# Weaving one token block's dense work between the expert row groups of the other block, in a two-block model on one core

## The chip, the cores and the metric

The kernel runs on one core of a Trainium2 chip. The metric is the device time of one launch, in microseconds (us), as the median of several runs. All data are float32. The core's engines are TensorE (PE, with its weight loads counted as PEld), VectorE (DVE), ScalarE (ACT), GpSimd (POOL) and SyncE (SP, which here issues transfers only); 16 DMA engines move data between the device's memory and the core's.

## What is computed

A batch of 256 tokens with 1024 features goes through two layers, each a mixer, then a product-key expert layer with 16 of 16384 experts for each of 8 heads, then a gated embedding (called PLE below), and after that through a second block (modulated norms, an attention of three branches, a stick-breaking attention, and a feed-forward of 2816 columns). The mixer of layer 0 is an mLSTM, that of layer 1 a latent attention (called MLA below). The expert layer is what fetches most data:

```python
def peer_ffn(x, w_q, sub_keys, u, v):
    q = (xt @ w_q).reshape(T, PEER_HEADS, 2, PEER_HALF)
    s = jnp.einsum('thcd,hcnd->thcn', q, sub_keys)
    s1, i1 = lax.top_k(s[:, :, 0], K)
    s2, i2 = lax.top_k(s[:, :, 1], K)
    ...
    top_s, top_pos = lax.top_k(cand_s, K)
    gates = jax.nn.softmax(top_s, axis=-1)
    ...
        ub = jnp.take(u, eb, axis=0)
        act = jax.nn.gelu(jnp.einsum('thkd,td->thk', ub, xb), approximate=False)
        vb = jnp.take(v, eb, axis=0)
        return jnp.einsum('thk,thkd->td', gb * act, vb)

    # first_block, for each of DEPTH = 2 layers i
        x = layer_norm(DN_ALPHA * x + mix, ln_g[i, 0], ln_b[i, 0])
        x = layer_norm(DN_ALPHA * x + peer_ffn(x, ...), ln_g[i, 1], ln_b[i, 1])
        x = x + jax.nn.sigmoid(x @ ple_w_gate[i]) * (p[i] @ ple_w_proj[i])
```

## The kernel before

Each engine runs a program written out by hand, and semaphores tie them together. So the order of the code is the order on the engine, and an engine that waits holds all that stands behind it. The 256 tokens are two token blocks (`tb` 0 and 1) of 128, one token to a partition.

**Expert rows.** A token uses 8 x 16 = 128 experts, so a block of 128 tokens has 128 gathers: each (L923, an indirect DMA that POOL issues) brings one row of 8 KB, an expert's u and v, to each partition. The four pairs of layer and block make 512 gathers. Eight row slots in `arena` (`gath`) hold them, handled in groups of two (`GRP`), four groups in flight. For a group DVE forms the two dot products with the token (L1517), ACT the gelu (`gelus`), DVE a diagonal matrix from identity, gelu and gate for each row (`diag`, L1523), and PE multiplies the diagonal by the v half of the row, 512 columns twice, into two PSUM banks (`mm`, L266), which stay open over all 128 rows. When PE is done with a row its slot is free for the next gather (`row_free`). L266 and L983 are the lines of the helpers for matmul and activation, so most PE and ACT work shows there, told apart by tiles and shapes.

**Choosing experts.** `peer(l)` first makes the queries of both blocks (16 groups of 128 columns, each for 256 tokens) and the scores. One choice (`choose`, DVE) serves two heads of one block, 32 experts, so a block has four (`UNITS`). In each layer the first two choices, both of block 0, come before the first dot product; the other six are laid in pieces, three after each group, into the rows of block 0. All weights come through `ring`, four slots of 2 MB (`take` on PE, issued by SP at L866 in the order in which PE takes them); SP waits for a slot until PE's last use of it.

**Order.** Layer 0's mixer; queries; rows of block 0; rows of block 1, with the PLE of block 0 among its first groups; then block 1's sum, norm and PLE, the MLA projections, attention and output projection of both blocks, queries of layer 1, with no rows; rows of layer 1 in the same way; PLE; the second block, here called the tail. The modulation of the tail needs products of a vector with 12 weight pieces of 512 columns (`in_w_ada`), which DVE multiplies (`ada_part`, L1307) and PE sums (`ada_sum`). Two of them (`ADA_COLS[4:6]`) stand at the output projection of the first mixer (`out_proj("mix0", ...)`), two (`ADA_COLS[6:8]`) at that of MLA, four elsewhere in the first mixer, four in the tail. The sum of the expert output with the residual is closed on PE and normed by DVE straight from PSUM.

## Time and profile before

| | |
|---|---|
| Median of 3 runs | 2393.95 us (2392.46 to 2401.32) |
| Profiled execution | 2393.88 us, its span 2392.1 us |
| PE, weight loads | 1994.0 us busy (83%), 1112.9 (47%) |
| DVE | 1355.6 us (57%) |
| ACT | 322.4 us (13%) |
| POOL | 583.3 us (24%) |
| DMA queue of the gathers (q0) | 540.13 MB, 55.0% of the engines' span |
| DMA queue of SP (q1) | 158.24 MB, 18.5% |
| Chain that ended last | PE 51%, DVE 23%, DMA 18% |

The profile is one execution of the program. Busy shares are means over a span whose stages differ, so the table alone doesn't tell what binds: that is read stage by stage, from the slices and from windows of the trace. PE's time contains matmuls at whatever clock was granted (PEclk, 1.00 is full), and a gather's time from issue to landing contains its wait behind other gathers. The gathers move 8 KB packets on one queue, the weights and vectors smaller packets on another, and both share the 16 DMA engines.

### The profile page before, as it was taken

How to read it: one execution, taken by the hardware profiler on the slowest of the kernel's cores; microseconds unless marked ns; L12 is line 12 of the kernel's file. 1: busy time of each engine (PE TensorE's matmuls, PEld its weight loads, DVE VectorE, ACT ScalarE, POOL GpSimd, SP SyncE). 2: the span in 40 equal slices, each digit the busy share in tenths (PEclk: the TensorE clock that was granted, in tenths of full speed). 3: DMA queues.
4: the chain of work that ended last, by engine and by line, in shares of the span. 5: the costliest groups of instructions: out<-in, count | busy, mean ns of one | idle time of the engine just before them, and what ended most of it. 6: DMA issues, size and time to landing. Idle time of an engine off the chain costs nothing.

```text
span 2392.1 us, 17529 instructions
## 1 busy us (share of the span) xinstructions
PE 1994.0 (83%) x6060; PEld 1112.9 (47%) x6060; DVE 1355.6 (57%) x3401; ACT 322.4 (13%) x776; POOL 583.3 (24%) x590
## 2 busy tenths in 40 slices
PE   8989777776987778989777776987777999989998
PEld 5447432332432224757432232432223877758863
DVE  3666689986566663366689986666664225420001
ACT  1111110100100001321010010100001216510000
POOL 1001344443444430001344443444432000000000
PEclk9999989899999998999989899999998989999999
DMA  7655999999999993535999999899994564233440
GB/s 262 225 193 196 393 411 401 377 393 397 369 405 422 421 421 121 200 109 221 373 410 390 392 381 422 350 397 422 421 422 160 167 220 149 78 141 112 144 176 35
DMA packets 148376, 699.49 MB, mean 292 GB/s; under 512 B 10880, under 2 KB 16064, under 8 KB 81728
## 3 DMA queue, kind: packets, MB, share of 16 engines
q0 software_dynamic: 74832, 540.13, 55.0%
q1 hardware_dynamic: 73456, 158.24, 18.5%
q8 instruction: 48, 0.79, 0.1%
q14 instruction: 40, 0.33, 0.0%
HBM read 697.28 MB, written 1.05 MB: 292 GB/s over the span
## 4 chain that ended last, share of the span: by engine, by line
PE 51%; DVE 23%; DMA 18%; ACT 3%; issue 2%; POOL 2%; DVEq 0%; POOLq 0%
PE bank L266 50%; DMA arena<-in_uv,eidx 18%; DVE arena L1517 9%; DVE sreg L1523 2%; DVE y_tok L1461 2%; POOL arena L923 2%; DVE y_tok L1457 2%; ACT glu L983 1%; DVE y_tok L1493 1%; DVE y_tok L1494 1%; DVE y_tok L1490 1%; ACT L983 1%; DVE sreg L1453 1%; ACT xT L983 1%; DVE y_tok L1453 0%
## 5 line engine op out<-in xcount | busy, mean ns | idle before, releaser
L266 PE MATMUL bank<-arena,sreg 128*128 128x512 f32 x2048 | 993.8, 636 | 318.2 <-DVE sreg L1523 317.8
L923 POOL DMA_INDIRECT arena<-in_uv,eidx x512 | 551.6, 1077 | 1165.8 <-PE bank L266 745.2
L266 PEld LDWEIGHTS bank<-arena,sreg 128*128 128x128 f32 x2048 | 396.4, 201 | 911.7 <-issue 465.1
L1517 DVE CUSTOM_DVE_ANT_0 arena<-arena,x_tok 128x1024 f32<-128x1024 f32 x512 | 619.0, 1224 | 260.7 <-DMA arena<-in_uv,eidx 258.1
L266 PE MATMUL bank<-xT,ring 128*128 128x256 f32 (+1 forms) x1984 | 447.3, 387 | 19.4 <-POOL identa L904 10.0
L266 PEld LDWEIGHTS bank<-xT,ring 128*128 128x128 f32 (+1 forms) x1984 | 379.2, 192 | 81.1 <-issue 16.1
L1523 DVE TENSOR_SCALAR sreg<-ident,glu,gate 128x128 f32<-128x128 f32 x512 | 162.3, 400 | 93.4 <-ACT glu L983 93.4
L983 ACT ACTIVATE glu<-dots 128x2 f32<-128x2 f32 x256 | 52.0, 203 | 1188.9 <-DVE dots L1517 1188.9
L266 PE MATMUL bank<-ring,xT 128*128 128x512 f32 (+4 forms) x480 | 189.6, 553 | 4.2 <-ACT xT L983 2.4
L266 PE MATMUL bank<-ring,arena 128*128 128x512 f32 x320 | 138.2, 593 | 2.6 <-ACT arena L983 2.0
L266 PEld LDWEIGHTS bank<-ring,xT 128*128 128x128 f32 x480 | 91.4, 201 | 97.0 <-issue 86.1
L983 ACT ACT_TABLE_LOAD x79 | 101.4, 1283 | 2.4 <-PEq L1908 0.8
L266 PEld LDWEIGHTS bank<-ring,arena 128*128 128x128 f32 x320 | 60.6, 190 | 78.0 <-issue 76.9
L983 ACT ACTIVATE arena<-bank 128x256 f32<-128x256 f32 (+5 forms) x118 | 50.0, 426 | 344.0 <-PE bank L266 340.4
L1848 DVE TENSOR_TENSOR arena<-arena,bank 128x256 f32<-128x256 f32 x22 | 9.3, 421 | 150.3 <-PE bank L266 150.3
L1307 DVE SCALAR_TENSOR_TENSOR ring<-ring,silu_cT 128x512 f32<-128x512 f32 x84 | 63.2, 752 | 3.0
L266 PE MATMUL bank<-arena,ring 128*128 128x256 f32 (+1 forms) x296 | 61.1, 370 | 0.7 <-ACT arena L983 0.7
L266 PE MATMUL bank<-arena 64*128 64x256 f32 (+6 forms) x304 | 56.0, 331 | 6.2 <-DVE arena L1399 4.9
L1836 DVE TENSOR_TENSOR y_tok<-bank,arena 128x512 f32<-128x512 f32 x8 | 5.5, 690 | 93.8 <-PE bank L266 93.8
L971 POOL TENSOR_SCALAR qreg<-qreg 128x384 f32<-128x384 f32 x8 | 9.3, 1167 | 198.9 <-DVEq L1767 198.7
L266 PEld LDWEIGHTS bank<-arena,ring 128*128 128x128 f32 x296 | 53.9, 202 | 7.8 <-issue 1.4
L266 PEld LDWEIGHTS bank<-arena 128*128 128x128 f32 (+2 forms) x304 | 43.1, 186 | 17.5 <-issue 7.8
(238 smaller groups left out, 969.5 us busy)
## 6 DMA issues: line engine op xcount, KB each, us to landing
ring<-in_w_ada SPq DMA_DIRECT2D x12, 2048.0 KB, 8.2
ring<-in_w_in_2r SPq DMA_DIRECT2D x10, 2048.0 KB, 11.8
ring<-in_peer_w_q SPq DMA_DIRECT2D x8, 2048.0 KB, 9.6
ring<-in_a_w_in SPq DMA_DIRECT2D x6, 2048.0 KB, 11.8
ring<-in_w_ffn_gate SPq DMA_DIRECT2D x5, 2048.0 KB, 7.8
ring<-in_w_ffn_up SPq DMA_DIRECT2D x5, 2048.0 KB, 11.0
ring<-in_w_ffn_down SPq DMA_DIRECT2D x5, 2048.0 KB, 7.9
arena<-in_uv,eidx POOLq DMA_INDIRECT x512, 11.5
```

What stands on the lines that cost most here:

```text
L266: return nc.tensor.matmul(o, l, r, start=start, stop=stop)
L923: pool.indirect_dma_start(gath[:, s, :], None, a["uv"], bass.IndirectOffsetOnAxis(ap=eidx[:, tb, it * SLOTS + s:it * SLOTS + s + 1], axis= ...
L983: return nc.scalar.activation(o, i, fn, **kw)
L1307: ins = v.scalar_tensor_tensor(w[:, k, :], w[:, k, :], scT[:, k:k + 1], w[:, k - 1, :], ALU.mult, ALU.add)
L1453: step.go(v.match_replace(scores[:, i, :], vals[:, i, 0:8], scores[:, i, :], -3.0e38))
L1457: step.go(v.max(vals[:, i, lo:lo + 8], scores[:, i, :]))
L1461: step.go(v.max_index(idx[:, i, lo:lo + 8], vals[:, i, lo:lo + 8], scores[:, i, :]))
L1490: step(v.tensor_tensor(eq, p12f[:, e, :, :].unsqueeze(3).broadcast_to([P, UH, 16, 16]), iota16[:, :].unsqueeze(1).unsqueeze(1).broadcast_t ...
L1493: step(v.tensor_tensor(eq, eq, i4[:, :, e, :].unsqueeze(2).broadcast_to([P, UH, 16, 16]), ALU.mult))
L1494: step(v.tensor_reduce(i12[:, e, :, :], eq, AX, ALU.add))
L1517: v.tensor_tensor_reduce(out=gath[:, s, 0:D], in0=gath[:, s, 0:D], in1=xt[:, tb, :], scale=1.0, scalar=0.0, op0=ALU.mult, op1=ALU.add, acc ...
L1523: v.tensor_scalar(diag[:, s, :], ident[:, :], glu[:, s:s + 1], gate[:, tb, c:c + 1], ALU.mult, ALU.mult).then_inc(sem("diag"), 1)
```

## The change

**A row's product turns round.** DVE no longer writes a diagonal. It multiplies gelu and gate of two rows (`coef`), ACT scales the v half of each row in place, and PE transposes it, eight 128 x 128 transposes a row that add up in the same two PSUM banks (L513, `is_transpose=True`). The sum is then feature-major: the residual is added by eight small matmuls, ACT moves it to `yt`, PE turns it back, and DVE norms it, with statistics and application in separate steps.

**One row of groups.** The four windows (layer 0 block 0, layer 0 block 1, layer 1 block 0, layer 1 block 1) follow each other with POOL gathering straight on. `weave` runs the same plan on PE, ACT and DVE: after the dots and the gelu of a group (`head`) come the dense slots that the plan puts there, then the product, the scaling and the transposes (`tail`).

- Window 0 carries block 1's queries and scores, and choices 1 to 7 of layer 0. Ahead of it stand only the queries of block 0 and choice 0.
- Window 1 carries, for block 0: layer 0's sum and norm, PLE, MLA projections, attention (the first 128 keys), output projection, queries of layer 1 and four choices. Window 2 carries the same for block 1, with 256 keys.
- Window 3 carries block 0's last sum, PLE and norm.
- Block 1's last sum, PLE and norm follow the rows, then the tail.

All of this is done for 128 tokens at a time, where the dense part was done for 256. So each weight from `pT_wp` to `peer_w_q` is now taken twice. The keys of the heads share a matmul shape of 128 columns; attention takes two heads at a time. PLE uses tanh of half the argument in place of the sigmoid.

**Modulation.** `ADA_COLS[4:8]` leave the two output projections for the tail: two stand at the compression matmuls, two in the attention loop. The regions `qreg` and `sreg` become `keep_region` and `work_region`, and `x_ready` and `xn_ready` become one semaphore for each block.

```diff
+PLAN = ((FIRST_SLOTS, 5, GROUPS - 4), (NEXT_SLOTS, 0, GROUPS - 2), (NEXT_SLOTS, 0, GROUPS - 2), (LAST_SLOTS, 0, 24))
+def weave(window, slots, head, tail):
+    n, lead, over = PLAN[window]
...
+        head(k)
+        upto = min(n, lead + -(-(k + 1) * (n - lead) // over))
+        while done < upto:
+            next(slots)
+            done += 1
+        tail(k)
...
 @block.tensor
-        out_proj("mix0", A["hT"], a["a_w_out"][0], ADA_COLS[4:6])
+        out_proj("mix0", A["hT"], a["a_w_out"][0])
...
+            def tail(k):
+                for e in range(GRP):
+                    s = (k * GRP + e) % SLOTS
+                    pe.wait_ge(sem("scaled"), r * PAIRS + k * GRP + e + 1)
+                    for c in range(KC):
+                        ins = nc.tensor.matmul(bank(f"pe{l}_{tb}_{c // 4}")[:, (c % 4) * P:(c % 4 + 1) * P],
+                                               gath[:, s, D + c * P:D + (c + 1) * P], ident[:, :],
+                                               start=k == 0 and e == 0 and c % 4 == 0, stop=False, is_transpose=True)
+                    ins.then_inc(sem("row_free"), 1)
...
+        for r, slots in enumerate((first_slots(), next_slots(0), next_slots(1), last_slots())):
+            start(r)
+            weave(r, slots, no_head, row_tail(r))
...
+        ada_load(ADA_COLS[4])
         w, rec = take(rows(w_in, 1536, 280), KC, 280)
...
+        ada_load(ADA_COLS[5])
         for kv in range(2):
             w, rec = take(a[f"cmp_w1_{'kv'[kv]}_2"][0].rearrange("(l p) m -> p l m", p=P), 16, P)
...
             last_use(rec, nm)
+            ada_sum(ADA_COLS[4 + kv])
...
 @block.scalar
+                act.wait_ge(sem("coef"), r * GROUPS + k + 1)
+                for e in range(GRP):
+                    s = (k * GRP + e) % SLOTS
+                    f(gath[:, s, D:2 * D], gath[:, s, D:2 * D], ACT.Copy, scale=coef[:, s:s + 1]
+                      ).then_inc(sem("scaled"), 1)
...
+            evac_T("xM", xT, tb)
+            act.dma_start(M["cg"], a["kvg"]).then_inc(sem("mla_par"), 16)
...
 @block.vector
-                for s in range(g * GRP, (g + 1) * GRP):
-                    c = it * SLOTS + s
-                    v.tensor_scalar(diag[:, s, :], ident[:, :], glu[:, s:s + 1], gate[:, tb, c:c + 1],
-                                    ALU.mult, ALU.mult).then_inc(sem("diag"), 1)
+                v.tensor_tensor(coef[:, s:s + GRP], glu[:, s:s + GRP], gate[:, tb, k * GRP:(k + 1) * GRP], ALU.mult
+                                ).then_inc(sem("coef"), 1)
```

The numbers of `PLAN` give, for each window, its slots, how many come before the rest is spread, and over how many of its 64 groups they are spread: 41, 78, 78 and 17 slots over 60, 62, 62 and 24 groups, five of the first window's 41 at its first group.

How that moves the instructions stands in the order of each engine (tile out <- tiles in, shape, count). PE before, from the rows of layer 0's block 0 (`arena,sreg`, four matmuls a row) to those of block 1, the closing sum (`x_tok,identa`), and the PLE of block 0 (`ring,xT` and `ring`):

```order
L266 MATMUL bank<-arena,sreg 128x512 x240
L266 MATMUL bank<-x_tok,identa 128x512 x2
L266 MATMUL bank<-arena,sreg 128x512 x16
L334 MATMUL bank<-ident,x_tok 128x128 x8
L266 MATMUL bank<-arena,sreg 128x512 x16
L266 MATMUL bank<-ring,xT 128x512 x8
L266 MATMUL bank<-ring 128x512 x2
L266 MATMUL bank<-arena,sreg 128x512 x16
L266 MATMUL bank<-ring,xT 128x512 x8
L266 MATMUL bank<-ring 128x512 x2
L266 MATMUL bank<-arena,sreg 128x512 x208
```

Behind it come 208 matmuls of rows with nothing between. PE after, at the same place (`ident,arena` are the rows' transposes, eight a row, sixteen a group; `ident,y_tok` is the turn of the sum):

```order
L513 MATMUL bank<-ident,arena 128x128 x736
L295 MATMUL bank<-identa,x_tok 128x128 x8
L513 MATMUL bank<-ident,arena 128x128 x16
L538 MATMUL bank<-ident,y_tok 128x128 x8
L513 MATMUL bank<-ident,arena 128x128 x48
L359 MATMUL bank<-ident,x_tok 128x128 x8
L513 MATMUL bank<-ident,arena 128x128 x16
L295 MATMUL bank<-ring 128x512 x4
L513 MATMUL bank<-ident,arena 128x128 x16
L295 MATMUL bank<-ring,xT 128x512 x4
L513 MATMUL bank<-ident,arena 128x128 x16
L295 MATMUL bank<-ring,xT 128x512 x8
```

A step of dense work now stands between almost every two groups, and it goes on like this to the window's end. SP before, the weights from layer 0's PLE to layer 1's queries, each once:

```order
L866 DMA ring<-in_pT_wp 128x2x1280
L866 DMA ring<-in_ple_w_gate 128x8x512 x2
L866 DMA ring<-in_kv_w_down_r 128x8x512
L866 DMA ring<-in_b_w_dq 128x8x384
L866 DMA ring<-in_kv_w_up 128x2x2048
L866 DMA ring<-in_b_w_uq_p 128x3x768 x2
L871 DMA lnp<-in_lnp 128x2048
L866 DMA ring<-in_b_w_out 128x8x512 x2
L866 DMA ring<-in_w_ada 128x8x512 x2
L866 DMA ring<-in_peer_w_q 128x8x512
L866 DMA ring<-in_keysT 128x2048
L866 DMA ring<-in_peer_w_q 128x8x512 x3
```

SP after, the same stretch for block 0:

```order
L992 DMA ring<-in_pT_wp 128x2x1280
L992 DMA ring<-in_ple_w_gate 128x8x512 x2
L992 DMA ring<-in_kv_w_down_r 128x8x512
L992 DMA ring<-in_b_w_dq 128x8x384
L997 DMA lnp<-in_lnp 128x2048
L992 DMA ring<-in_kv_w_up 128x2x2048
L992 DMA ring<-in_b_w_uq_p 128x3x768 x2
L992 DMA ring<-in_b_w_out 128x8x512 x2
L992 DMA ring<-in_peer_w_q 128x8x512 x2
L992 DMA ring<-in_keysT 128x2048
L992 DMA ring<-in_peer_w_q 128x8x512 x2
```

Then the same eleven rows follow once more, for block 1; the modulation's loads are gone from here. They stand in the tail, SP after:

```order
L992 DMA ring<-in_w_in_2r 128x8x512
L992 DMA ring<-in_w_ada 128x8x512
L992 DMA ring<-in_w_in_2r 128x8x280
L992 DMA ring<-in_w_ada 128x8x512
L992 DMA ring<-in_cmp_w_k 128x16x128
L992 DMA ring<-in_cmp_w_v 128x16x128
```

Before, the two compression weights (`cmp_w`) followed the `w_in` loads of 512 and 280 columns directly; now a load of `in_w_ada` stands ahead of the 280 columns and another ahead of the compression weights.

## Rows read from the trace of the kernel before

**Rows 1.** The page, part 2: granted clock and GB/s in 40 slices of 59.8 us.

```profile
PEclk9999989899999998999989899999998989999999
...
GB/s 262 225 193 196 393 411 401 377 393 397 369 405 422 421 421 121 200 109 221 373 410 390 392 381 422 350 397 422 421 422 160 167 220 149 78 141 112 144 176 35
```

**Rows 2.** Stretches: length, then busy us by engine, clock granted, DMA share, GB/s.

```profile
core 0: us, PE busy (x) PEld busy (x) DVE busy (x) ACT busy (x) POOL busy (x), PEclk, DMA share, GB/s
...
270.00:580.00 310.00, 234.83 (x465) 93.78 (x464) 260.09 (x715) 29.85 (x77) 128.18 (x116) 0.91 0.98 401
...
705.00:900.00 195.00, 144.24 (x312) 56.05 (x312) 120.44 (x235) 7.93 (x39) 79.01 (x78) 1.00 1.01 421
912.00:1110.00 198.00, 179.55 (x689) 126.34 (x688) 87.13 (x239) 45.61 (x111) 1.15 (x2) 0.93 0.37 133
...
1812.00:2392.00 580.00, 541.33 (x2250) 403.47 (x2250) 146.00 (x335) 118.23 (x256) 19.66 (x45) 0.96 0.37 132
```

**Rows 3.** DMA queues from 208.6 to 912: packets, MB, share of 16 engines.

```profile
DMA packets 40279, 276.32 MB, mean 393 GB/s; under 512 B 4160, under 2 KB 4160, under 8 KB 7488
...
q1 hardware_dynamic: 3392, 7.60, 2.9%
```

**Rows 4.** The same two queues from 275 to 300.

```profile
q0 software_dynamic: 1065, 7.73, 74.9%
q1 hardware_dynamic: 1282, 2.57, 27.3%
```

**Rows 5.** The weights' queue alone, from 300 to 330.

```profile
q1 hardware_dynamic: 913, 1.83, 16.1%
```

**Rows 6.** The gathers, line L923, over the run, from issue to landing.

```profile
DMA to landing us min/median/max: 5.5/11.5/17.7
```

**Rows 7.** The page, part 5: line, engine, tiles, shapes, count | busy, mean ns | idle.

```profile
L1517 DVE CUSTOM_DVE_ANT_0 arena<-arena,x_tok 128x1024 f32<-128x1024 f32 x512 | 619.0, 1224 | 260.7 <-DMA arena<-in_uv,eidx 258.1
...
L1523 DVE TENSOR_SCALAR sreg<-ident,glu,gate 128x128 f32<-128x128 f32 x512 | 162.3, 400 | 93.4 <-ACT glu L983 93.4
L983 ACT ACTIVATE glu<-dots 128x2 f32<-128x2 f32 x256 | 52.0, 203 | 1188.9 <-DVE dots L1517 1188.9
...
L983 ACT ACT_TABLE_LOAD x79 | 101.4, 1283 | 2.4 <-PEq L1908 0.8
```

**Rows 8.** ACT's groups by shape, same columns.

```profile
L983 ACT ACTIVATE sreg<-bank 128x512 f32<-128x512 f32 x16 | 9.6, 597 | 8.2 <-PE bank L266 8.2
...
L983 ACT ACTIVATE arena<-arena 128x1024 f32<-128x1024 f32 x5 | 5.0, 1046 | 0.0
```

**Rows 9.** PE in order of time: start, us, line, tiles, shape, count [idle before].

```profile
136.40 27.70 PE L266 MATMUL bank<-ring,arena 128*128 128x512 f32 x64 [1.03 <-ACT arena L983]
...
173.13 16.64 PE L266 MATMUL bank<-xT,ring 128*128 128x256 f32 x64 [0.99 <-ACT xT L983]
...
254.10 4.63 PE L266 MATMUL bank<-ring,qreg 128*128 128x128 f32 x40
...
919.90 1.94 PE L334 MATMUL bank<-ident,x_tok 128*128 128x128 f32 x8 [3.26 <-DVE y_tok L1276]
...
927.83 1.04 PE L334 MATMUL bank<-ident,x_tok 128*128 128x128 f32 x8
```

**Rows 10.** DVE in order of time, one expert choice, first and last instruction.

```profile
192.30 0.87 DVE L1457 MAX8 y_tok<-sreg 128x8 f32<-128x128 f32 x4 [18.99 <-ACT sreg L983]
...
208.17 0.18 DVE L1499 TENSOR_SCALAR eidx<-y_tok 128x32 uint32<-128x32 f32 x1
```

**Rows 11.** PE and DVE after the last rows, in order of time.

```profile
1854.52 5.48 DVE L1307 SCALAR_TENSOR_TENSOR ring<-ring,silu_cT 128x512 f32<-128x512 f32 x7
...
1857.30 29.76 PE L266 MATMUL bank<-xT,ring 128*128 128x256 f32 x128 [4.44 <-ACT xT L983]
...
1886.90 1.02 PE L266 MATMUL bank<-ring,ones 128*128 128x512 f32 x2
```

**Rows 12.** A stretch with a pause of the rows, columns as in rows 2.

```profile
1470.00:1500.00 30.00, 18.47 (x34) 7.47 (x33) 19.54 (x36) 3.58 (x7) 7.29 (x7) 0.77 0.87 364
```

More of the change, by code:

```diff
@@ L635, in _ @@
+        transposes("xT6", yt, KC, 1, xn_ready[1], 1)
+        for tb in range(TB):
+            await_T("xT6", tb)
         w_in = a["w_in_2r"]
```

1469 lines of the change are left out of this document (865 added, 604 removed).

## The prediction

> **What bounds the kernel now.** Read the slices first, for what is moved and when [rows 1]. They split the 2392.1 us span into five stretches. The slices near 400 GB/s are the expert rows of the two layers; in between and at the end stand dense stretches at 100 to 240 GB/s. The first choice of experts ends at 208.4 [rows 10] and the gathers start there. The rows run to 912, a dense stretch of 198 us follows (attention and its projections), the second layer's rows run from 1110 to 1812, and a dense tail of 580 us closes [rows 2].
>
> Now ask what ends last in a stretch of rows. From 705 to 900, with nothing beside them, the rows move 421 GB/s at a DMA share of 1.01, while PE is busy 144 of 195 us and DVE 120: the transfers are the limit [rows 2]. A gather brings 128 rows of 8 KB, 1.05 MB, so 2.49 us; 195 us are 78 rows (312 matmul records, four to a row). Where DVE also chooses experts (270 to 580: DVE busy 260 of 310 us) 401 GB/s remain, 5% less though DVE is not full [rows 2]. That 5% is what uneven demand costs when two limits lie close, and I use it below. Over 208.6 to 912, 276.32 MB took 703 us, where 421 GB/s would take 656 [rows 3].
>
> So there is a cheap resource in each place: the DMA engines between the layers (share 0.37 in 912 to 1110), and PE and ACT among the rows [rows 2]. The change runs the rows of the four (layer, block) windows in one row, and lays the dense stretch between their groups of two rows.
>
> **First gather.** The first choice no longer needs the queries of both blocks. The 16.64 us of 256-column matmuls before the first scores [rows 9] become 8.3, and they start some 6 us earlier: two sums of the modulation on PE (1.02 each, [rows 11]) and the wait for block 1's norm are gone from their front. 8.3 + 6 is 14, so 208 becomes 194. The two DVE parts that are dropped there lay beside the output projection (27.70 us, [rows 9]) and give nothing.
>
> **One row, each engine.** DVE: the dot stays 1.224 us, the 0.400 us diagonal goes [rows 7], and one tiny product for two rows comes (no row shows it; between nothing and 0.4, I take 0.2). ACT gains a scaling of 1024 columns; the nearest row is 1.046 us [rows 8]. PE: four records of 512 columns, 144.24/78 = 1.85 us a row [rows 2], become eight transposes, 1.04 us in a running stream, 1.94 after a pause [rows 9]. A group of two rows therefore needs 2.65 us of DVE, 2.1 + 0.2 of ACT, 2.1 to 3.9 of PE, against 5.0 us of transfers. Rows alone stay bound by the transfers: nothing is gained or lost there.
>
> **What windows 1 and 2 carry beside 128 rows each.** PE: 40 matmuls of 512 columns at 27.70/32 = 0.87 us (35 us), sixteen of 256 and 384 (9), 252 of 128 columns at 4.63/20 = 0.23 us (58) [rows 9], 45 transposes (6): 108 us, plus 133 for the rows. DVE: 157 for the dots, 13 for products, 64 for four choices of 16.05 us [rows 10], about 30 for norms, rotation and softmax: 264. ACT: 134 + 13 for rows and gelus, about 25 for evacuations at 0.6 [rows 8], and eleven square roots or exponentials that each force two table loads of 1.283 us (28) [rows 7]: 200. Transfers: 128 gathers, 319 us, and weights that are now fetched once for each block: 29.4 MB. The weight queue moved 2.57 MB in 27.3% of 25 us, 377 GB/s [rows 4], so 78 us. The sum is 397 us, and it is the largest of the four.
>
> But each group ties the engines together. DVE does dots, then the slots' work, then the product; ACT must gelu before and scale after; PE does its slot before the transposes. A plan of 78 slots in 62 groups puts two slots into every fourth group, and there ACT often waits for what PE makes in the same group (PE free again about 3.3 us after the last product, 3.7 for a 128-column projection slot, evacuation 0.6 to 1.2, scaling 2.1): 8.5 to 9 us, against 5.3 for a group with one slot. In the first 49 groups that is 6.1 us on average, and the transfers (244 of the gathers' 319, 58 of the weights' 78) are 6.2: two limits at the same place, a little worse than in 270 to 580, so I take 8% over 302, 326 us. In the last 15 groups the choices lie on DVE: 2.45 + 0.2 + 19 slots of 3.2 over 15 groups, 6.7 us, against 5.0 + 1.3 of transfers; with the 5%, 106. Together 432; bounds are 397 (no loss) and 480 (every slot exposed to 2.5 us more). For the clock I add 2: [rows 12] show 0.77 granted where the rows paused, and PE would rest more often than it does now.
>
> **Windows 0 and 3.** Window 0: 319, plus 18.1 MB (queries, keys and norm of block 1; first four weights of the next) 48, plus a pause: the eight first gathers have landed by about 216, while gates 0 wait on ACT behind the remaining query columns and DVE makes choice 1 (16 us) before its first dot, so that the first slot is free at 229, 13 us later; 3% for the six choices spread over it, 10. 390. Window 3: 319 + 7.6 MB (20) + 6: 345.
>
> **Rows in all:** 390 + 434 + 434 + 345 = 1603 us, from 194 to 1797, against 1812 now. The hidden 198 us are spent again: on weights fetched twice (60 MB more in the windows, 160 us) and on losses in windows 1 and 2 (35 each).
>
> **Tail.** The last sum now goes through PSUM, ACT, and PE again before the norm: +3; half of the first evacuation with the norm's scale is done in window 3: -3. Four modulation columns move here from places where they were covered. Each is 6 us on DVE and 1.0 on PE [rows 11] and holds one of four weight slots until PE has summed it. On SP, the second compression weight waits for the slot of column 4, whose sum stands behind the first compression matmul; so PE idles about 8 us there, and the first compression weight comes some 7 us later than PE could use it: +16 with the sums. The other two sit in the attention loop, where PE is full: 2 for PE, 6 for DVE's bursts, 1 at the end. 580 becomes 605 (bounds: 580, if SP keeps ahead; 620).
>
> **Sum:** 194 + 1603 + 605 = 2402; the profiled execution took 1.8 us more than its span (2393.88 to 2392.1), so **2404 us**. That is 0.4% over both it and the median of 2393.95; about 0.5% is what can be told from no change.
>
> **Rivals.** *The transfers stay saturated.* If the four groups in flight absorb the doubled slots, windows 1 and 2 take 397 + 8 each, window 0 380, window 3 339, the tail 600. For it: a landing took 5.5 us at least and 11.5 in the median [rows 6], so the pipeline has some 6 us of slack in a group. Against it: the 5% of 270 to 580 with lighter slots. 194 + 1529 + 600 = 2323 (2295 to 2370).
>
> *PE's clock stays low.* It ends on the slower side. The row work turns wholly into transposes. If a stretch of transposes does not hold the granted clock at 1.00, a group costs 3.9 us of PE, and a dense slot behind it starts at half clock: 3.3 us on average becomes about 5.8. 34 groups with such slots take 7.9 us and 30 take 3.9: 386 us of PE beside 397 of transfers, and with the same latencies stretched, about 465 for each window; window 0 takes 5 more. 2404 + 62 + 5 = 2471 (2440 to 2510). It decides once PE's rest after a group keeps the clock down in windows 1 and 2; in 0 and 3 it costs nothing, 3.9 being under 5.0. For it: after a pause the eight transposes took 1.94 [rows 9], and the clock was 0.77 at 18.47 of 30 us busy [rows 12]. Against it: at 74% busy the clock was 1.00, and PE in windows 1 and 2 would be busy for 241 of 434 us. The Trainium skill, "TensorE: Matmul & The Clock Gate", Part 4: PE-mode transpose, says that a transpose does not count as PE activity for the gate; no row here shows a long stretch of transposes, so neither is settled.
>
> *Weights come too slowly.* Beside saturated gathers the weight queue got 2.57 MB in 25 us, 103 GB/s, and later 1.83 in 30, 61 GB/s [rows 4, 5]. 29.4 MB need 285 us at the one rate, 482 at the other, and PE waits at the head of its queue, with all rows behind it. At 61 GB/s each middle window is about 48 us longer: 2500. Against it: a waiting PE drains the gathers, which gives the weights the engines. The Trainium skill, "DMA: Bandwidth & Descriptors", Queues, rings and completion order, says that an engine takes turns between queues packet by packet; small weight packets beside row packets of 8 KB get the small share that rows 4 show, and by it alone the first rate would hold, so this rival would not.
>
> **Chances.** Forecast 0.46 (2370 to 2440: 0.10 faster by over 0.5%, 0.22 within, 0.14 slower); saturated transfers 0.22; clock 0.20; weights 0.08; other waits, slower, 0.04. Faster 0.32, same 0.22, slower 0.46. The range of 2310 to 2490 leaves out the ends of the first and last rivals, below 2 in 10.
>
> **What would show it.** First gather near 194. Windows 1 and 2 near 434 us each: GB/s of 390 to 400 with long runs of 421 speaks for the first rival; a clock near 0.5 to 0.7 there, with eight transposes at 1.94 us, for the second; PE waiting for ring slots with gathers idle, for the third. In the tail, a PE gap before each compression matmul. I am wrong most where groups cost other than 5.3 and 9 us, or where the two row windows' boundary stalls.

## The result

The changed kernel takes 2322.85 us (median of 4 runs, 2322.32 to 2323.57), the kernel before 2396.16 beside it: a ratio of 0.9694, with a 95% interval of 0.968 to 0.9708. It is 3% faster. The forecast was 2404 us, and a slowdown was held likelier than a gain. The first rival, saturated transfers, gave 2323.

The page after, part 2, in 40 slices of 58 us (answers to [rows 1]): granted clock, DMA share in tenths, GB/s.

```profile
PEclk9998976777888886788888778777789699999999
DMA  7637999999999999999999999999974552344340
GB/s 273 229 127 308 384 400 413 413 397 422 391 417 413 416 415 408 400 390 416 413 417 415 407 370 409 416 421 421 421 289 163 202 197 109 109 145 145 109 181 36
```

The valley in the middle of [rows 1] (121, 200, 109 GB/s) is gone: from slice 5 to slice 29 the DMA engines are full. The next view cuts the same trace where the rows begin and where each window's sum is formed, so its lines are the four windows and the tail. Columns as in [rows 2].

```profile
core 0: us, PE busy (x) PEld busy (x) DVE busy (x) ACT busy (x) POOL busy (x), PEclk, DMA share, GB/s
193.60:578.70 385.10, 220.88 (x1383) 202.13 (x1382) 279.49 (x813) 185.35 (x234) 151.87 (x134) 0.77 1.00 403
578.70:979.20 400.50, 281.50 (x1688) 240.14 (x1687) 250.09 (x650) 198.01 (x274) 142.42 (x128) 0.82 1.01 408
979.20:1384.30 405.10, 291.40 (x1710) 245.53 (x1710) 254.99 (x654) 199.33 (x274) 144.64 (x128) 0.82 1.00 404
1384.30:1715.40 331.10, 203.80 (x1098) 170.97 (x1097) 175.29 (x334) 161.12 (x204) 162.09 (x162) 0.77 0.99 410
1715.40:2321.00 605.60, 553.34 (x2272) 413.64 (x2270) 170.95 (x393) 119.53 (x257) 11.46 (x11) 0.93 0.40 144
```

Read the DMA share first: 1.00, 1.01, 1.00, 0.99. DVE is busy 62% of window 1 and PE 70%; neither is full. In the same cut the forecast had this:

| term | predicted us | measured us |
|---|---|---|
| first gather | 194 | 193.6 |
| window 0 | 390 | 385.1 |
| window 1 | 434 | 400.5 |
| window 2 | 434 | 405.1 |
| window 3 | 345 | 331.1 |
| tail | 605 | 605.6 |

So 62 of the 81 us by which the sum was too high lie in windows 1 and 2, and nothing in the two ends.

The gain can be counted in full. Before, the stages were 208.6, 703.4 (rows), 198 (dense), 702 (rows) and 580 us. After, they are 193.6, 1521.8 (rows) and 605.6. The first gather gives 15 us, the dense stretch 198, and the tail takes 26 back. The rows take 1521.8 instead of 1405.4, 116 us more. What fills these 116 us shows in the transfers' queues of the four windows (answers to [rows 3]):

```profile
DMA packets 107885, 617.88 MB, mean 406 GB/s; under 512 B 9040, under 2 KB 11664, under 8 KB 40864
...
q0 software_dynamic: 73872, 537.04, 86.0%
q1 hardware_dynamic: 33360, 79.17, 13.6%
```

The weights' queue moves 79.2 MB among the rows, where it moved 7.6 in each of two stretches. Price it by the queue's own share: 13.6% of 1521.8 us is 207 us, where 2.9% of 1405 was 41 [rows 3], so these 64 MB more cost 166 us. The gathers' packets take 1309 us against 1306, and what is not listed here 3 more. Against them stands the idle time of the DMA engines among the rows: it was 4% of 1405 us in the kernel before (0.96 in both stretches), 57 us, and is now 1 or 2. 166 + 3 + 3 - 56 is 116, which is the difference measured.

The groups of instructions that changed (answers to [rows 7]):

```profile
L513 PE MATMUL bank<-ident,arena 128*128 128x128 f32 x4096 | 696.9, 339 | 471.3 <-ACT arena L1092 471.1
...
L1710 DVE CUSTOM_DVE_ANT_0 arena<-arena,x_tok 128x1024 f32<-128x1024 f32 x512 | 622.2, 1224 | 440.7 <-DMA arena<-in_uv,eidx 437.2
L1092 ACT ACTIVATE arena<-arena,coef 128x1024 f32<-128x1024 f32 x512 | 560.0, 1141 | 265.1 <-DVE coef L1721 260.1
```

DVE's dots now wait 437 us for gathers, where they waited 258: the engines ahead of the rows are waiting for the transfers more than before, with more work beside them.

### The profile page after: what moved, and what is told of

Its sections match the earlier page's. It is cut to its first block, busy times and chain, and to the rows that moved or that the text cites. A ratio compares the mean times of both kernels' runs of the same rounds, so it can differ in the third digit from the quotient of the medians.

```text
span 2321.0 us, 23416 instructions
## 1 busy us (share of the span) xinstructions
PE 1725.9 (74%) x8852; PEld 1383.2 (60%) x8852; DVE 1227.5 (53%) x3136; ACT 892.8 (38%) x1293; POOL 621.4 (27%) x587
## 4 chain that ended last, share of the span: by engine, by line
PE 45%; DMA 29%; DVE 13%; ACT 5%; POOL 4%; issue 3%; another core or an unknown queue 1%; SPq 0%; DVEq 0%; POOLq 0%
PE bank L295 36%; DMA arena<-in_uv,eidx 26%; PE bank L513 9%; DVE arena L1710 4%; POOL arena L1040 3%; ACT arena L1092 3%; DMA ring<-in_peer_w_q 2%; DVE y_tok L1643 1%; DVE y_tok L1639 1%; DVE y_tok L1676 1%; DVE y_tok L1677 1%; DVE y_tok L1673 1%; ACT L1092 1%; DMA ring<-in_cmp_w_k 1%
## 5 line engine op out<-in xcount | busy, mean ns | idle before, releaser
L513 PE MATMUL bank<-ident,arena 128*128 128x128 f32 x4096 | 696.9, 339 | 471.3 <-ACT arena L1092 471.1
L513 PEld LDWEIGHTS bank<-ident,arena 128*128 128x128 f32 x4096 | 615.9, 178 | 556.1 <-ACT arena L1092 543.2
L1040 POOL DMA_INDIRECT arena<-in_uv,eidx x512 | 587.0, 1147 | 1085.6 <-PE bank L513 828.4
L1092 ACT ACTIVATE arena<-arena,coef 128x1024 f32<-128x1024 f32 x512 | 560.0, 1141 | 265.1 <-DVE coef L1721 260.1
L295 PE MATMUL bank<-xT,ring 128*128 128x256 f32 (+2 forms) x2528 | 459.0, 344 | 48.0 <-DMA ring<-in_peer_w_q 31.6
L295 PEld LDWEIGHTS bank<-xT,ring 128*128 128x128 f32 (+1 forms) x2528 | 405.8, 196 | 94.7 <-issue 31.7
L295 PE MATMUL bank<-ring,arena 128*128 128x512 f32 x240 | 103.5, 593 | 1.6 <-ACT arena L1092 1.0
L1092 ACT ACTIVATE work_region<-bank 128x512 f32<-128x512 f32 (+3 forms) x80 | 38.6, 502 | 112.2 <-PE bank L295 80.7
L1721 DVE TENSOR_TENSOR coef<-glu,gate 128x2 f32<-128x2 f32 x256 | 41.0, 160 | 69.7 <-ACT glu L1092 66.6
L295 PE MATMUL bank<-ring,work_region 128*128 128x128 f32 (+1 forms) x208 | 55.2, 412 | 1.1 <-issue 0.7
```

Source lines behind the costliest of these rows:

```text
L295: return nc.tensor.matmul(o, l, r, start=start, stop=stop)
L513: ins = nc.tensor.matmul(bank(f"pe{l}_{tb}_{c // 4}")[:, (c % 4) * P:(c % 4 + 1) * P], gath[:, s, D + c * P:D + (c + 1) * P], ident[:, :], ...
L1040: pool.indirect_dma_start(gath[:, i % SLOTS, :], None, a["uv"], bass.IndirectOffsetOnAxis(ap=eidx[:, tb, i:i + 1], axis=0)).then_inc(sem(f ...
L1092: return nc.scalar.activation(o, i, fn, **kw)
L1721: v.tensor_tensor(coef[:, s:s + GRP], glu[:, s:s + GRP], gate[:, tb, k * GRP:(k + 1) * GRP], ALU.mult).then_inc(sem("coef"), 1)
```

## The experiments

Two theories stood. **Theory S**: in the windows the transfers are the limit, and the groups in flight absorb the slots. **Theory C**, the prediction's: the groups' chain over DVE, ACT and PE is as long as the transfers, and where two limits meet some per cent are lost. A time that is given without a ratio or an interval is that of a single execution; repeated executions of one kernel lie within 11 us of each other.

### The engines alone

```diff
-  pool.indirect_dma_start(gath[:, i % SLOTS, :], None, a["uv"], ...)
+  pool.indirect_dma_start(gath[:, i % SLOTS, 0:D], None, a["uv"].rearrange("r (h n) -> (r h) n", h=2), ...)
-  f(gath[:, s, D:2 * D], gath[:, s, D:2 * D], ACT.Copy, scale=coef[:, s:s + 1])
+  f(gath[:, s, D:2 * D], gath[:, s, 0:D], ACT.Copy, scale=coef[:, s:s + 1])
```

> The changed kernel, but each gather brings 4 KB (1024 of 2048 columns of a row, of another row than the reference's) and ACT scales the product of the dot in place of the v half: same instructions on PE, DVE and ACT, half the gathers' bytes; the output is not the reference's. It shows what the engines alone take. Theory C (the prediction's groups of 5.3 and 9 us): windows 1 and 2 take about 400 us each, window 0 330, window 3 200: 2130 us. Theory S (the groups overlap, DVE's 251 busy us of window 1 are next): 290 us each, window 0 300, window 3 190: about 1870 us.

2046.67 us. The four windows of this run:

```profile
193.70:513.70 320.00, 207.05 (x1384) 190.38 (x1384) 276.14 (x815) 185.61 (x234) 146.36 (x134) 0.82 0.79 271
513.70:860.30 346.60, 266.43 (x1687) 226.66 (x1687) 246.56 (x650) 198.28 (x273) 148.35 (x128) 0.85 0.78 278
860.30:1204.60 344.30, 263.81 (x1712) 221.60 (x1711) 250.12 (x652) 199.79 (x274) 145.74 (x128) 0.89 0.78 279
1204.60:1438.80 234.20, 163.83 (x1098) 132.54 (x1097) 171.54 (x335) 160.95 (x204) 159.65 (x159) 0.94 0.86 300
```

Both theories missed. The DMA share is now below 0.8, so the engines' chain shows: 346 us for a middle window, where the prediction's groups of 5.3 and 9 us summed to 400 and the rival's guess was 290. That is 5.4 us a group, not 6.24, and 54 us under the 400 of the transfers in the changed kernel. The 54 us are not spread evenly. Window 1 cut at DVE's first instruction of a choice, in the changed kernel and then in this run:

```profile
578.70:853.00 274.30, 206.92 (x1244) 172.54 (x1243) 139.35 (x285) 136.63 (x197) 99.31 (x88) 0.86 1.01 410
853.00:979.20 126.20, 74.58 (x446) 67.59 (x445) 110.74 (x368) 61.38 (x77) 43.11 (x40) 0.73 1.00 404
```

```profile
513.70:739.90 226.20, 188.67 (x1190) 155.98 (x1190) 135.50 (x284) 134.99 (x195) 101.24 (x86) 0.91 0.82 295
739.90:860.30 120.40, 77.75 (x499) 70.69 (x498) 111.06 (x367) 63.29 (x79) 47.11 (x42) 0.73 0.71 247
```

Ahead of the choices 48 us go with half of the gathers' bytes; there the two limits do not meet. From the first choice on only 6 us go, at a DMA share of 0.71: there the engines need nearly as long as the transfers, and DVE is busy for 111 of 120 us. Window 3, 3.66 us a group where DVE needs 2.65, has yet another limit, which is not shown: POOL issues gathers for 160 of its 234 us, and it waits 45 us for a free slot.

### Fewer rows in flight

```diff
-        pe.sem_inc(sem("row_free"), SLOTS)
+        pe.sem_inc(sem("row_free"), 6)
```

(and 4 in the second run, with the last wait on `row_free` changed to fit.)

> The changed kernel with six rows (three groups) in flight instead of eight. Theory S (four groups in flight absorb the long groups): three groups are 7.5 + 7.5 us of transfers; a row goes round in some 12 us (landing 5.5 at least, dots 2.4, gelu and product 0.4, scaling 2.3, transposes 1 to 2), so groups without a slot still fit in 15 us, doubled ones do not: windows 1 and 2 lose 10 to 30 us each, 2350 to 2390 us in all. If the weave did not need the depth: 2323.

> The changed kernel with four rows (two groups) in flight. Theory S: two groups are 10 us of transfers against some 12 us of a row's way round without slots and 15 or more with them, so every group costs at least 6 us and a group with slots 7.5: windows 0 and 3 about 450 and 400, windows 1 and 2 about 500: 2600 to 2700 us. If depth is not what hides the slots: under 2450.

2499.92 and 3093.29 us: six rows cost 177 us, four cost 770, far over what was expected of either. Window 3 alone, where hardly a slot stands, with six rows and then with four:

```profile
1513.50:1892.00 378.50, 218.76 (x1099) 186.19 (x1098) 175.38 (x333) 160.78 (x204) 151.43 (x164) 0.70 0.93 359
```

```profile
1959.70:2485.40 525.70, 237.92 (x1098) 204.27 (x1097) 177.83 (x337) 160.85 (x204) 150.54 (x166) 0.63 0.71 262
```

With two groups in flight a group takes 525.7/64 = 8.2 us, so a slot goes round in 16.4 us; with three, 5.9 and 17.7. The rival on record spoke of "some 12 us". The gathers' landing in the run with four is most of it:

```profile
DMA to landing us min/median/max: 6.7/8.0/13.7
```

8.0 for the landing, 1.25 until the pair's second gather is issued, 2.4 for the dots, 0.5 for gelu and product, 2.2 for the scaling and some 2 for the transposes make 16.4. With eight slots the loop allows a group every 4.1 to 4.4 us, and the transfers ask for one every 5.0. For rows alone the depth is just enough: it leaves some 3 us in 20. In windows 1 and 2 it leaves more. With two groups in flight window 1 took 581.1 us, so a slot with the dense work in its way goes round in 18.2 us, while the transfers of four groups take 25.0 there (four times 400.5/64). Three groups' transfers take 18.8, and with six rows window 1 was 39 us longer.

### The weights' transfers

In window 2 each weight load brings an eighth of its columns.

```diff
+                if r.get("light"):
+                    dst, src = dst[:, :, 0:r["n"] // 8], src[:, :, 0:r["n"] // 8]
```

> The changed kernel, but in window 2 (block 1's dense work among layer 1, block 0's rows) each weight load brings an eighth of its columns, so 25.7 of 29.4 MB are not moved and the rest of each ring slot is stale; the output is not the reference's. Theory S (the transfers are the limit in the woven windows): the window, 404 us in the changed kernel's profile at 404 GB/s, loses 25.7 MB / 408 GB/s = 63 us, so about 341 us, the other windows as they were, about 2260 us in all. Theory C (as predicted, the groups' engine chain is as long as the transfers, 6.1 us for a group): the window stays above 390 us, over 2310 in all.

2284.13 us; window 2 fell from 405.1 to 365.3. That is outside both numbers. Its DMA queues tell why the 63 us were wrong for window 2:

```profile
DMA packets 29995, 145.09 MB, mean 397 GB/s; under 512 B 10270, under 2 KB 10910, under 8 KB 13470
...
q1 hardware_dynamic: 11408, 11.37, 9.2%
```

The weights' queue moved 11.4 MB in the window, not 3.7, because the next windows' first weights and the norms' parameters are fetched there in full; the changed kernel moved 28.57. 17.2 MB at 408 GB/s are 42 us, and 39.8 were won. The DMA share was still 1.00.

The first light weights of window 2 are fetched in window 1, at its end, under the choices. Window 1 moved 6.7 MB less (22.71 for 29.36), 16 us by theory S, and took 402.5 us, no less than the 400.5 of the changed kernel. Its choices, to set beside the stretch from 853.00 above:

```profile
852.30:979.20 126.90, 77.11 (x444) 69.96 (x443) 111.42 (x369) 61.50 (x77) 42.89 (x40) 0.70 0.93 353
```

The share fell to 0.93 and the time stayed at 126.9. So theory S holds in its mechanism and its rate ahead of the choices. In the choices the engines, DVE first among them, are as long as the transfers, and the bytes taken away there won nothing in window 1.

### Not woven, and woven more tightly

```diff
-PLAN = (..., (NEXT_SLOTS, 0, GROUPS - 2), (NEXT_SLOTS, 0, GROUPS - 2), ...)
+PLAN = (..., (NEXT_SLOTS, NEXT_SLOTS, 1), (NEXT_SLOTS, NEXT_SLOTS, 1), ...)
```

> The changed kernel, with all 78 slots of windows 1 and 2 laid before the first group of their window instead of one or two after each group (and one more wait on DVE between two rotations). Theory S: what hides the dense work is the weave alone; each of the two windows takes its 319 us of gathers plus a dense stretch of about 200 us less the eight rows that are in flight (20), about 500 instead of 402: 2520 us. Rival: the gain comes from the early first gather and the smaller row work, and the weave hides little beside twice the weights: under 2420 us.

2580.06 us. Windows 1 and 2 take 522 and 539 instead of 401 and 405:

```profile
580.30:1102.70 522.40, 313.63 (x1687) 259.78 (x1686) 257.72 (x652) 187.06 (x261) 156.45 (x128) 0.76 0.78 314
1102.70:1641.60 538.90, 331.38 (x1711) 269.54 (x1710) 262.82 (x656) 188.89 (x262) 154.83 (x128) 0.75 0.76 305
```

The rival falls: the dense work laid in a lump costs 256 us more than woven, with the same instructions but for one wait on DVE, and with the same bytes. The kernel is then slower than the kernel before. In either window the gathers stand still while the lump runs. From 590 to 780 POOL issues none, and what the DMA engines move is weights and the rows already asked for:

```profile
590.00:780.00 190.00, 125.25 (x637) 95.98 (x637) 79.32 (x311) 29.64 (x63) 0.00 (x0) 0.78 0.45 162
```

The other plan puts two slots into each of 39 groups:

```diff
-PLAN = (..., (NEXT_SLOTS, 0, GROUPS - 2), (NEXT_SLOTS, 0, GROUPS - 2), ...)
+PLAN = (..., (NEXT_SLOTS, 0, 39), (NEXT_SLOTS, 0, 39), ...)
```

> The changed kernel with the 78 slots of windows 1 and 2 spread over 39 groups instead of 62, so two slots in each of them. Theory C: each such group takes 8.75 us, 341 for 39 and 125 for the 25 others, 466 a window: 2450 us. Theory S: only the groups with two choice slots (DVE 2.45 + 0.2 + 6.4 = 9.05 us against 5.0 to 6.3 of transfers, ten of them, less 6 us of slack) lose, some 25 us a window: 2370 us.

2353.86 us: windows 1 and 2 take 419.9 each, 19 and 15 more. Theory C's 466 is out; theory S had 25. The DMA share is 0.97 over window 1, and the trace tells where it is lost. Two stretches of it:

```profile
786.00:807.00 21.00, 16.01 (x141) 15.45 (x140) 15.25 (x54) 10.72 (x15) 5.28 (x5) 1.00 0.68 245
849.00:880.00 31.00, 16.24 (x94) 13.93 (x92) 25.01 (x76) 16.18 (x20) 10.60 (x10) 0.73 0.71 259
```

They account for some 16 of the 19 us. Ahead of the first PE waited 9.0 us for a weight of the queries, with the rows behind it, and no gather was issued for 18.6 us. Ahead of the second stand the groups with two choice slots: between 815 and 870 POOL issues a pair of gathers every 9.1 us, which is the 9.05 of the expectation.

### PE's clock and the transposes

> The changed kernel, with the rows' eight transposes as ordinary matmuls against the identity, same tiles and count. Granted clock over the four windows is 0.79 in the changed kernel. If it is low because transposes do not hold it, it rises to 0.90 or more, with PE's records of the rows shorter on the mean (339 ns now); if it is low because PE rests after each group, it stays at 0.75 to 0.83. Theory S: the time stays within 5 us of 2323 either way, since PE is not the limit. A theory by which the low clock costs time: 2300 or less if the clock rises.

```diff
-   start=k == 0 and e == 0 and c % 4 == 0, stop=False, is_transpose=True)
+   start=k == 0 and e == 0 and c % 4 == 0, stop=False)
```

2384.27 us (0.996 of the kernel before, interval 0.9949 to 0.9972): 61 us slower than the change, where no difference was expected. The ordinary matmul of float32 leaves two records for each transpose's one (8192 against 4096), so this run changed PE's load as well as its kind. The next keeps the kind and takes the load: every transpose is issued twice.

> The changed kernel with each of the rows' transposes issued twice into the same place; the output is not the reference's (the rows' sum counts double). The ordinary matmuls of the run before made two records for each transpose's one, so PE's load is now the same as there (clock 0.95 to 0.98 in the windows), with transposes only. If the granted clock follows PE's busy share whatever the instruction, it is 0.9 or more in the windows, and the windows are some 20 us longer as there (2385 us). If transposes do not hold the clock, it stays at 0.8 or below, with PE's records longer and windows longer still: over 2400 us.

```diff
-                    for c in range(KC):
+                    for c in [c for c in range(KC) for _ in range(2)]:
```

2382.19 us. One stretch in window 1 and one in window 3, of the changed kernel, of the ordinary matmuls and of the transposes twice, in this order:

```profile
600.00:960.00 360.00, 259.07 (x1533) 220.96 (x1533) 224.81 (x601) 173.75 (x244) 123.51 (x112) 0.81 1.01 410
1500.00:1680.00 180.00, 107.08 (x583) 92.52 (x583) 96.07 (x184) 89.56 (x112) 89.51 (x73) 0.76 1.01 421
```

```profile
600.00:960.00 360.00, 320.63 (x2380) 291.95 (x2379) 202.72 (x512) 168.78 (x238) 117.32 (x108) 0.95 0.97 391
1500.00:1680.00 180.00, 147.06 (x1145) 133.88 (x1144) 92.21 (x176) 82.91 (x106) 78.08 (x69) 0.99 1.01 418
```

```profile
600.00:960.00 360.00, 314.64 (x2382) 284.38 (x2381) 206.46 (x525) 170.06 (x239) 122.41 (x110) 0.95 0.98 395
1500.00:1680.00 180.00, 141.69 (x1121) 127.34 (x1120) 92.80 (x177) 83.91 (x107) 80.17 (x69) 0.98 1.01 417
```

The last two kernels are alike in time, load and clock. In window 3 PE does almost nothing but transposes, and with twice of them the granted clock rises from 0.76 to 0.98. So transposes hold the clock as ordinary matmuls do, and the low clock of the changed kernel comes from PE's rest. The Trainium skill, "TensorE: Matmul & The Clock Gate", Part 4: PE-mode transpose, says that a transpose does not count as busy PE in the same way; this measurement speaks against it for float32 transposes of 128 x 128, and decides. The low clock costs nothing among the rows: in window 3 of the changed kernel the transfers run at 421 GB/s at 0.76. What costs is PE work in the loop: two more microseconds of it in each group (32 records of 0.12 us instead of 16) made windows 0 to 2 some 15 to 22 us longer each, and window 3 only 2 to 5.

### The modulation columns

The tail was forecast to grow by 16 us where a column's load stands ahead of each compression weight. Waits of PE in the tail of the changed kernel:

```profile
PE bank L295 <- DMA ring<-in_cmp_w_k: 8.2, 1, 8.2
PE bank L295 <- DMA ring<-in_cmp_w_v: 6.5, 1, 6.5
```

Three kernels move the two columns away. First, into the attention loop, beside the two that are there:

```diff
-        ada_load(ADA_COLS[4])
...
-        ada_load(ADA_COLS[5])
...
-            ada_sum(ADA_COLS[4 + kv])
...
+                ada_load(ADA_COLS[4 + ch // 4])
...
+            if h % 2 == 1:
+                ada_sum(ADA_COLS[4 + h // 2])
...
+            if h % 2 == 0:
+                ada_part(ADA_COLS[4 + h // 2])
+                if h:
+                    ada_column(ADA_COLS[3 + h // 2])
```

> The changed kernel with modulation columns 4 and 5 moved from the compression matmuls into the attention loop of the tail, where 6 and 7 stand already; one load, one product and one sum at each of four places of the loop. In the changed kernel PE waits 8.2 and 6.5 us for the two compression weights. If these waits come from the columns' loads and ring slots standing ahead (the step of the prediction), they go, and the tail is 12 to 15 us shorter: 2308 to 2311 us. If DVE's bursts hold up the attention loop instead, 2 to 6 of it comes back.

2332.01 us (0.9735 of the kernel before, interval 0.9718 to 0.9753), so slower than the change. The two waits went, and this one came, in the attention loop:

```profile
PE bank L295 <- DVE ada_columns L1497: 16.5, 3, 5.5
```

PE's sum of a column keeps its bank until DVE reads it, and DVE read it after its next 5.5 us product. Second, with the two in the other order:

> As the run with columns 4 and 5 in the attention loop (its tail was 614.7 us, PE waiting 16.5 us in three places for DVE to free the bank of a column's sum), but DVE reads each sum before it starts the next column's 5.5 us product instead of after it. If those three waits came from that order alone, they go: tail about 598 us, 2315 us in all. If DVE's bursts hold up the attention loop in any order, the tail stays over 606.

2320.35 us (0.9694, interval 0.9676 to 0.9713), tail 603.4: the three waits are gone, 11 us come back, but PE now waits 9.4 us in four places for the softmax that DVE's products hold up. The expectation was 2315. Third, back to the first mixer's output projection, as in the kernel before:

```diff
-        out_proj("mix0", A["hT"], a["a_w_out"][0])
+        out_proj("mix0", A["hT"], a["a_w_out"][0], ADA_COLS[4:6])
...
+        for j in ADA_COLS[4:6]:
+            ada_part(j)
         for tb in range(TB):
             residual("mix0", tb, 0)
...
+        for j in ADA_COLS[4:6]:
+            ada_column(j)
```

> The changed kernel with modulation columns 4 and 5 back at the first mixer's output projection, as in the kernel before. The tail loses the two waits for the compression weights (8.2 and 6.5 us) and two sums of 2.05: 606 becomes about 588. The first gather comes 2 to 6 us later than at 193.6 (two sums of 1.02 us ahead of the queries, and weights of the queries behind two more loads). In all 2306 to 2312 us. If the first gather slips by more than 10 us, the change had moved the columns at no cost.

2300.92 us (0.9605, interval 0.9581 to 0.9629), and the tail 582.8. The first gather came at 191.1, no later than at 193.6 but earlier. PE in order of time, columns as in [rows 9], first in the changed kernel, then in this one:

```profile
165.61 9.01 PE L295 MATMUL bank<-xT,ring 128*128 128x128 f32 x64 [2.98 <-ACT xT L1092]
```

```profile
160.74 1.88 PE L295 MATMUL bank<-ring,ones 128*128 128x512 f32 x4
...
164.75 7.38 PE L295 MATMUL bank<-xT,ring 128*128 128x128 f32 x64 [1.26 <-ACT xT L1093]
```

The two sums fill PE's pause between the projection and the queries, and the queries take 7.38 us, against 9.01 in the changed kernel. So this part of the change was a loss of 22 us, not of 16. The two waits are 14.7 of them. Much of the rest is PE's clock behind the waits. The two compression matmuls in the changed kernel, then both together in this run:

```profile
1816.88 7.04 PE L295 MATMUL bank<-arena,ring 128*128 128x32 f32 x32 [8.23 <-DMA ring<-in_cmp_w_k]
...
1832.25 7.04 PE L295 MATMUL bank<-arena,ring 128*128 128x32 f32 x32 [6.47 <-DMA ring<-in_cmp_w_v]
```

```profile
1810.61 8.21 PE L295 MATMUL bank<-arena,ring 128*128 128x32 f32 x64
```

From 1815.4 to 1840.4 the changed kernel's granted clock was 0.50, half of the full one. The 64 records took 14.1 us where they take 8.2 now, 6 us more, and each of the two sums took 2.05 us where the forecast had 1.0.

### Window 0: bytes or start

The first layer's queries and scores of both blocks are made ahead of window 0, each weight loaded once:

```diff
+        pq_both(1, 0)
+        for j in range(1, 4):
+            pq_both(0, j)
+            pq_both(1, j)
+            scores(0, 0, j)
+            scores(0, 1, j - 1)
+        scores(0, 1, 3)
```

> The changed kernel, with block 1's queries and scores of layer 0 made ahead of window 0 from the same weights as block 0's, so that window 0 loads 9.4 MB less. Theory S (window 0 lasts as long as its bytes take): 9.4 MB / 408 GB/s = 23 us less, 362 instead of 385, about 2300 us in all; the first gather stays near 194 since only choice 0 stands ahead of it. Rival (window 0 is set by its start, where the first rows wait for choice 1 and the queries, and by DVE's choices): within 8 us of 2323.

2318.73 us (0.969, interval 0.9672 to 0.9708). Window 0 fell from 385.1 to 374.7, 10 of 23 us. Its transfers from 194 to 560, in 40 slices of 9.15 us:

```profile
DMA  9930599999999999999999999999999999999999
GB/s 339 424 158 0 198 394 416 414 411 423 419 423 416 425 383 349 413 424 424 401 419 424 414 384 395 427 406 425 418 392 381 424 425 372 427 420 398 420 427 420
```

The fourth slice stands still and its neighbours run at less than half: the first eight gathers have landed, and POOL issues the ninth at 242.4; what ends the pause at 234 is the first weight of window 1. In the changed kernel the queries' weights filled this gap. So taking 9.4 MB away won only what did not lie in the pause. Two more kernels: both edits together, and both with the last queries laid as slots behind the first groups, so that ACT reaches the first gelu earlier.

> The changed kernel with both edits: modulation columns 4 and 5 at the first mixer, and the first layer's queries made once for both blocks. If the two are independent (22 us and 4 to 11 us), 2290 to 2297 us; window 0 about 375, the tail 583.

```diff
+                if 5 <= i < 9:
+                    pq_half(0, (i - 5) // 2, 3, (i - 5) % 2)
+                for at, tb, j in ((8, 0, 3), (9, 1, 2), (10, 1, 3)):
+                    if i == at:
+                        scores(0, tb, j)
```

> As the run with both edits, but the fourth query weight's matmuls of both blocks and the last scores are laid as slots behind the first groups, so that ScalarE reaches the first gelu some 16 us earlier. If window 0's start is what kept 13 of the 23 us, the first row's transposes start near 224 instead of 240 and window 0 takes 360 to 366 us: 2280 to 2288 us. If window 0 has another limit (DVE's choices, 112 us of them beside the dots), it stays above 370 and the time above 2290.

2290.92 us (0.9559, interval 0.9535 to 0.9582) and 2289.92 (0.957, interval 0.9554 to 0.9586). The edits add up. The spread start hardly shows: the first scaling comes at 224.1, where it came at 240.0 in the run with both edits (33.2 and 44.4 us after the first gather), but window 0 is 372.6 against 374.0. From where the transfers are full again to the window's end, the two traces read, in this order:

```profile
234.00:569.00 335.00, 185.63 (x1041) 167.89 (x1041) 256.16 (x720) 179.16 (x222) 140.85 (x126) 0.75 1.00 406
```

```profile
230.00:563.00 333.00, 189.87 (x1117) 172.24 (x1116) 250.85 (x697) 172.84 (x215) 138.82 (x126) 0.76 1.00 410
```

Both are full for the same 333 to 335 us. Where the 11 us of an earlier scaling went, the issues tell. In the run with both edits the first weight of window 1 and the ninth gather are issued at

```profile
236.46 0.37 SPq L996 DMA_DIRECT2D ring<-in_pT_wp  x1
245.22 1.57 POOL L1044 DMA_INDIRECT arena<-in_uv,eidx  x1 [39.78 <-PE bank L529]
```

and in the spread one the ninth gather comes first, with that weight at 264.4:

```profile
229.25 0.95 POOL L1048 DMA_INDIRECT arena<-in_uv,eidx  x1 [28.51 <-PE bank L528]
```

So the gathers resume 11 us sooner, counted from the first gather, but the transfers only 2.5: 38.3 us after it against 40.8, since weights had ended the pause before. These two kernels are the fastest here, 4.3% under the kernel before and 1.4% under the change.

## Why the prediction was wrong

**What bounds the rows: right, and read half.** The transfers were named as the limit, at 421 GB/s and share 1.01, and they stayed it. But the "5% less though DVE is not full" of [rows 2] was taken from GB/s (401 against 421). The same row has a DMA share of 0.98 against 1.01: 3% was idle, and the rest goes with smaller packets of weights. The changed kernel moves 403 to 408 GB/s in windows 0 to 2 at a share of 1.00 to 1.01. A rule made from the wrong column was then used for all four windows.

**First gather, 194: right** (193.6), with its working.

**One row, each engine: right in the durations.** ACT's scaling took 1.14 us, the dot 1.224, the tiny product 0.16.

**Windows 1 and 2, 434 each: the step that failed.** The sum of the transfers was 397 and they took 400.5 and 405.1. Two things stood on top of it. The group costs of 5.3 and 9 us put the engines' chain at 400 us a window, beside the transfers; it measures 346 with half the gathers' bytes away. It is the groups ahead of the choices that were too dear, at 299 us for 49 groups where 226 were measured up to the first choice; the choices were priced at 101 us for 15 groups, and from the first one on 120 were measured. And the 8% and 5% for two limits at one place measure as next to nothing, even in the choice groups, where DVE and the DMA engines are both full. In the changed kernel:

```profile
900.00:960.00 60.00, 31.39 (x144) 27.97 (x144) 57.49 (x188) 27.04 (x34) 18.81 (x18) 0.61 1.02 411
```

DVE is busy 57.5 of 60 us and the transfers run at 1.02. Both limits are real there, since neither half the gathers' bytes nor 6.7 MB of weights taken away shortened the choices of window 1 by more than 6 us. The loss is the mis-sized term, 35 us a window by the prediction and 4 to 8 measured over 397; the mis-sized chain is what made it look due.

**Window 0, 390: near in size, not in its terms** (385.1). The gathers' pause was there, with the ninth issued at 242.5 where the text had a slot free at 229, but the queries' weights filled it; a pause of the gathers costs only if nothing else wants to be moved. The pause and the 3%, 23 us, were not lost. The gathers' packets took 338 us (87.8% of the window) for 131 gathers, instead of 319 for 128, and the weights' 46 instead of 48.

**Window 3, 345: 14 too high.** Its weights were 4.2 MB and 11 us (3.3% of the window), not 7.6 MB and 20, the rest having come in window 2. The gathers' packets took 316 us, for 125 of the 128, and 3 or 4 us were idle, where the text had 319 and 6.

**Tail, 605: right in size** (605.6), and in the cause and length of the two waits (some 7 and about 8 us; 8.2 and 6.5). That the sum fits is in part luck. The two columns at the compression weights cost 22.8 us of tail where the text had 16, because the clock behind the waits was left out. What else was changed leaves 582.8, only 3 us over the 580 before, where the text had 9 for the other two columns. Nor was the price of the alternative right: the two columns could have stayed where they were at less than nothing.

**The rivals.** Saturated transfers (0.22) is what happened, and its sum of 2323 is within 1 us. It took a slack of "some 6 us" from the landings, which is near the 7 that windows 1 and 2 have (18.2 us a round trip in 25.0); rows alone have only 3. That it hits to 1 us is luck: its window 3 was 8 us too high and its middle windows 4, its window 0 and its tail 5 and 6 too low. PE's clock did stay low, at 0.77 to 0.82, and cost nothing there, since PE was never the limit among the rows; that it "decides once PE's rest keeps the clock down" was the wrong condition, and the transposes were not its cause. Both this rival (465 us a middle window) and that of slow weights (482) are excluded by the 400 and 405 measured. In window 1 the weights' queue moved 29.4 MB in 400 us and PE waited once for a weight, 5.4 us. The Trainium skill, "DMA: Bandwidth & Descriptors", Queues, rings and completion order, has the engines take turns between queues packet by packet; the trace does not contradict it, and no run here tests it.

**The chances.** 0.46 stood on a forecast whose own text named a sum of 397 and then added a loss found in another stage. With 3% in place of the 8 and the 5, the same working gives some 415 us a window and about 2366 in all (an estimate from its own terms), still 43 too high, 19 of it in windows 0 and 3.

## What to carry to other kernels

Read how full the DMA engines are from their share, and use GB/s only to price bytes: mixed packet sizes lower the one without freeing the other. When a prediction adds a loss for limits that lie close, look for a stretch in which both are full, and add nothing without one. Take bytes away only where the transfers are the limit alone: 17 MB less won 40 us in one window, and 6.7 MB less under the choices of another won nothing. Work that moves from a stage with idle transfers into one where they are the limit costs its bytes (here 64 MB more, 166 us), and the stage that it leaves must be worth more (here 198 us, and 56 of idle share). And before going round, count a buffer's round trip: 16.4 us against the 20 of four groups' transfers costs nothing, 17.7 against the 15 of three costs 177 us in all.

## What the runs showed of the hardware

Transposes of float32 on PE hold the granted clock like ordinary matmuls: 0.98 with PE busy 142 of 180 us on them, 0.76 with 107 of 180. An ordinary float32 matmul of 128 x 128 leaves two records of the same length as the transpose's one, so a transpose costs half of it. Two queues with 8 KB and smaller packets shared the DMA engines at a share of 0.99 to 1.01 over four windows, 1500 us, without a loss that the trace shows. A load of an eighth of the columns makes as many packets as the full one: window 2 had 11408 with 11.4 MB as with 28.6 MB, at 9.2% of 365 us against 18.3% of 405. And where PE waited 8.2 and 6.5 us for weights the granted clock was 0.50 over 25 us, with PE busy for 17 of them, so two waits of 14.7 us together, with the two sums behind them, cost 22.
